# Plain 256-column runs instead of four-element pieces in the gate and query products of a two-block transformer kernel

## What is computed

```python
def odd_layer(h, norm_g, w_in, rpb, w_out):
    b, L, _ = h.shape
    u = rmsnorm(h, norm_g)
    proj = jnp.einsum("bld,de->ble", u, w_in)          # 272 x 2048 by 2048 x 8192
    q, k, v, z = split_cols(proj, (NA_WIDTH,) * 4)
    shp = (b, L, NA_HEADS, NA_HEAD_DIM)
    o = neighbourhood_attention(q.reshape(shp), k.reshape(shp), v.reshape(shp), rpb)
    o = o.reshape(b, L, NA_WIDTH) * jax.nn.silu(z)
    return h + jnp.einsum("ble,ed->bld", o, w_out)
...
    h = rmsnorm(h, final_norm_g)
    return h[:, N_META:]
```

## Time and profile before

| | before |
|---|---|
| median of three runs | 2334.29 us |
| the profiled execution | 2334.73 us |
| its span in the trace | 2332.9 us |
| PE busy | 2311.9 us (99%) |
| PE weight load busy | 2192.8 us (94%) |
| DVE busy | 1801.6 us (77%) |
| ACT busy | 1198.6 us (51%) |
| GpSimd (POOL) busy | 583.8 us (25%) |
| HBM read | 434.88 MB, 191 GB/s over the span |

### The profile page before, as it was taken

One profiled execution on the slowest core, in us unless ns is written; L12 is line 12 of the kernel. 1 busy time (PEld: TensorE's weight loads), 2 busy tenths in 40 slices (PEclk: granted clock), 3 DMA queues, 4 the chain that ended last, 5 costly groups with the idle time before them and its releaser, 6 DMA issues.

```text
span 2332.9 us, 51145 instructions
## 1 busy us (share of the span) xinstructions
PE 2311.9 (99%) x17404; PEld 2192.8 (94%) x17404; DVE 1801.6 (77%) x3189; ACT 1198.6 (51%) x1735; POOL 583.8 (25%) x421
## 2 busy tenths in 40 slices
PE   9999999999999999999999999999999999999997
PEld 9999888888888888899999999999999999999997
DVE  7777888888888766689888889989873566666666
ACT  5444455555555444457666743343544444444444
POOL 0230000000000000013423368888788211111100
PEclk9999999999999999999999999999999999999999
DMA  8544656666665666655555545555555554555444
GB/s 312 187 166 145 200 199 209 207 204 205 202 209 201 211 197 195 193 186 194 178 187 173 189 169 180 180 180 198 175 180 180 191 174 164 169 169 180 160 164 152
DMA packets 152908, 438.19 MB, mean 188 GB/s; under 512 B 32387, under 2 KB 47148, under 8 KB 152700
## 3 DMA queue, kind: packets, MB, share of 16 engines
q1 hardware_dynamic: 149276, 424.42, 53.7%
q0 software_dynamic: 3264, 12.41, 2.0%
q10 hardware_dynamic: 288, 0.30, 0.0%
HBM read 434.88 MB, written 11.09 MB: 191 GB/s over the span
## 4 chain that ended last, share of the span: by engine, by line
PE 85%; DVE 8%; issue 3%; ACT 3%; DVEq 1%; DMA 0%; ACTq 0%; SPq 0%
PE bank L1194 24%; PE bank L1177 15%; PE bank L1179 14%; PE bank L1178 14%; PE bank L1195 12%; DVE wlo L1657 2%; DVE c L2084 1%; ACT whi L680 1%; DVE bank L2310 1%; PE bank L1440 1%; PE bank L1560 1%; PE bank L1550 1%; PE bank L1540 1%; PE bank L1567 0%; ACT L663 0%
## 5 line engine op out<-in xcount | busy, mean ns | idle before, releaser
L680 ACT CAST whi<-raw 128x1024 fp32r<-128x1024 f32 x784 | 817.2, 1048 | 508.1 <-PE bank L1179 359.1
L1657 DVE TENSOR_TENSOR wlo<-raw,whi 128x1024 fp32r<-128x1024 f32 x624 | 761.8, 1226 | 224.7 <-ACT whi L680 210.9
L1177 PE MATMUL bank<-xhl,whi 128*128 128x272 f32 (+1 forms) x3024 | 859.3, 284 | 1.2 <-DVE nvt L2456 0.4
L1179 PE MATMUL bank<-xhl,wlo 128*128 128x272 f32 (+1 forms) x3024 | 848.9, 281 | 0.0
L1178 PE MATMUL bank<-xhl,whi 128*128 128x272 f32 (+1 forms) x3024 | 848.6, 281 | 0.0
L1177 PEld LDWEIGHTS bank<-xhl,whi 128*128 128x128 f32 x3024 | 567.7, 188 | 5.1 <-issue 2.2
L1178 PEld LDWEIGHTS bank<-xhl,whi 128*128 128x128 f32 x3024 | 567.8, 188 | 0.6 <-issue 0.2
L1179 PEld LDWEIGHTS bank<-xhl,wlo 128*128 128x128 f32 x3024 | 567.6, 188 | 0.0
L1194 PE MATMUL bank<-xhl,whi 128*128 128x512 f32 x1408 | 469.9, 382 | 0.3 <-DVE ug L1987 0.3
L618 POOL TENSOR_TENSOR wlo<-raw,whi 128x1024 fp32r<-128x1024 f32 x160 | 381.5, 2392 | 94.9 <-ACT whi L680 94.8
L1195 PE MATMUL bank<-xhl,wlo 128*128 128x256 f32 x1408 | 384.4, 273 | 0.0
(11 more groups left out here) (292 smaller groups left out, 2781.4 us busy)
## 6 DMA issues: line engine op xcount, KB each, us to landing
raw<-w_up SPq DMA_DIRECT2D x176, 512.0 KB, 4.3
raw<-w_na SPq DMA_DIRECT2D x128, 512.0 KB, 3.6
raw<-w_ssm SPq DMA_DIRECT2D x96, 512.0 KB, 3.7
raw<-w_glu SPq DMA_DIRECT2D x96, 512.0 KB, 3.6
raw<-w_down SPq DMA_DIRECT2D x80, 512.0 KB, 3.7
raw<-w_qkv SPq DMA_DIRECT2D x48, 512.0 KB, 3.7
raw<-w_mix SPq DMA_DIRECT2D x32, 512.0 KB, 3.7
raw<-w_outa SPq DMA_DIRECT2D x32, 512.0 KB, 3.6
```

Source lines behind the costliest of these rows:

```text
L680: A.copy(whi[s][:, :], raw[s][:, :]).then_inc(sem("hi_done"), 1)
L1177: T.matmul(to_, wh, xh_, start=head, stop=False)
L1179: ins = T.matmul(to_, wl, xh_, start=False, stop=last)
L1657: V.tensor_tensor(wlo[s][:, :], raw[s][:, :], whi[s][:, :].bitcast(F32), SUB).then_inc(sem("lo_done"), 1)
```

## The change

In `product`, the products of stage `na` whose width is 256 (the gates and the queries) are now read from `xhl` and summed in PSUM in one plain run of 256 columns. Before, they were walked by lines. The values and keys of that stage (272 columns) and all other stages are as before. No instruction is added or removed, and no wait.

```diff
--- before.py
+++ after.py
@@ -1172,7 +1172,7 @@
                     wh, wl = whi[s][:, r * P:r * P + P], wlo[s][:, r * P:r * P + P]
                     head, last = start and n_ == 0, stop and n_ == len(kts) - 1
                     to_, xh_, xl_ = out, mh[:, o:o + n], ml[:, o:o + n]
-                    if phase not in ("pin", "qkv"):
+                    if phase not in ("pin", "qkv") and (phase, n) != ("na", SEQ):
                         to_, xh_, xl_ = by_lines(to_), by_lines(xh_), by_lines(xl_)
                     T.matmul(to_, wh, xh_, start=head, stop=False)
                     T.matmul(to_, wh, xl_, start=False, stop=False)
```

## The result

The changed kernel takes 2343.10 us (median of 8 runs, 2341.75 to 2344.85), the kernel before 2336.07 us (median of 8, 2333.92 to 2338.63; its first three runs were those shown ahead of the prediction). The ratio is 1.0031, with a 95% interval of 1.0022 to 1.0039. The change makes the kernel slower by about 7 us, outside the range that was predicted. The profiled execution took 2343.36 us with a span of 2341.6, 8.7 us more than the span before.

What follows compares the result with a forecast made beforehand. PE was taken as the bound, so time follows matmul steps. A gain of 0.105 us a pass over 16 passes gave 1.7 us, taken as 1.6: 2334.29 - 1.6 = 2332.7 us (median), range 2331.5 to 2338.0.

Steps and rivals of the forecast that it cites:

- What bounds the kernel: PE busy without a gap in `na` at full clock, so each ns won per matmul is won on the path.
- What a plain run costs: Plain 256-column matmuls in `na` take 113.3 ns each as in `pin`, or 117.7 in the slow rhythm of `qkv`.
- the chunk after the transposes: 24 matmuls in each `na` pass after line 1550: 2.82 to 2.84 us against 2.84, gain taken as 0.005 us.
- Rival 2: Run of 72 in `na` locks in the slow rhythm: 3.2 us slower, 4.4 with slow chunk; chance 0.18.
- 8.47 us means rival 2: Sign in PE's timeline: 72-runs of `na` at 8.47 us, not the forecast 8.17, would show the slow rhythm.
- the last sentence of the prediction: Forecast is wrong if the plain run's step is neither 113.3 nor 117.7 ns, or if PE begins to wait.
- Rival 1: Quick run of 72 but slow chunk after the transposes in `na`: gain 0.5 us, no change, 2334.0 us; chance 0.27.
- Rival 3: Following stage `naout` falls to the slow pair rhythm: some 210 pairs at 9.2 ns more, 1.9 us; chance 0.07.
- Rival 4: Plain run in `na` cheaper than in `pin`, without the fixed 6.7 ns: gain 12.4 us, 2321.9; chance 0.01.
- whole cachelines: Walking costs nothing in itself, since four elements at a time are whole 8-byte PSUM cachelines.
- The range: Kernel time from 2331.5 to 2338.0 us, put at 0.84; the forecast's own part 2331.5 to 2333.5.

Runs made afterwards that it cites:

- one_line_lower: Changed kernel with the plain gates and queries of `na` read from one line (16 columns) lower, tokens 0 to 255; 2338.24 us, ratio to before 1.0014.
- sums_only_walked: Changed kernel with only the PSUM sums of the gates and queries walked by lines, columns read plainly; 2342.49 us in one run.
- reads_only_walked: Changed kernel with only the reading of the gates' and queries' columns walked by lines, sums written plainly; 2337.60 us in one run.
- weights_up_a_line: Changed kernel with the two weight rings moved up one line (64 bytes) against all other tiles; 2361.79 us, ratio 1.011.
- columns_up_a_line: Changed kernel with the activations of the later layers laid one line further up in their tile; 2341.36 us in one run.

## Why the prediction was wrong

**What bounds the kernel** held. PE has no gap in the stage in either kernel, the clock is the same, and each ns a step went straight into the time: 16 x 0.52 = 8.3 us of the 8.7 us that `na` grew by.

**What a plain run costs** is the step that failed. I read 113.3 ns in `pin` and, in `qkv`, the two rhythms of 113.3 and 117.7, and put them on `na` as all that a plain run can do. But all 30 entries that I went through lie in one tile at one distance from the weights, three lines and so odd. They were 30 samples of one case. The run in question starts at an even distance. The shift by one line alone takes the run of 72 in `na` from 8.65 to 8.48 us and 72 steps of `pin` from 8.16 to 8.54. That `T0` is three lines where `LINES` is two stood in the code that I had read. The term was 16 x (8.17 - 8.27) = -1.6 us and measured 16 x (8.65 - 8.27) = +6.1 us; the chunk after the transposes was put at a gain of 0.005 us a pass and measured 16 x (2.96 - 2.84) = +1.9 us. The sample was thin in another way too: lines 1262 and 1268, which gave the quick rhythm only, gave the slow one three times in the same `qkv` in the trace of after.

**Rival 2** had the right place and the right form, a steady slow rhythm that the walked reading doesn't fall into, but not the cause: it made it a matter of the entry. Its price was the slow rhythm of the wrong distance: 4.4 us at the most. The line "8.47 us means rival 2" would have read as neither; the last sentence of the prediction, a step that is neither 113.3 nor 117.7, is what came. Its argument against, that the 272s run without a collision and so PE enters without one, didn't help: the 120 ns came after those 272s and after the transposes (2.96 us), and after plain 272s it was still 118.6.

**Rival 1** was right that the run and the chunk can differ (one_line_lower has 117.8 and a quick chunk), the other way round. **Rival 3** didn't come: `naout` kept its rhythm. (It has 240 pairs and not some 210, so its price should have been 2.2 us.) Its half of the idea, that pairs know two rhythms, is seen in `mix`. **Rival 4** is refuted by the result. By the Trainium skill's rule ("PSUM — Partial Sum Buffer", specifications) the change would have been a gain. That it cost 7 us could have hidden a gain on the writing side; `sums_only_walked` and `reads_only_walked` exclude it. The reason that the prediction gave, whole cachelines, was tried by no run.

**The range** was too narrow for one reason: it took the worst row of a sample as the worst case. What no row showed was a plain run at this distance, and I had noted that only for the entry.

**What stays open.** What picks between the rhythms of one distance isn't settled. `one_line_lower` and `weights_up_a_line` lock the run of 72 at 117.8 ns, `columns_up_a_line` at 113.3, all three at an odd distance, and the second of them has both in one trace. Counted on a grid of four lines from the weight rings, `columns_up_a_line` and `weights_up_a_line` even stand at the same place, three lines, so a coarser grid of four doesn't explain it. Nor is it shown why 256 plain columns are quick at an odd distance and 272 aren't; 272 plain columns at an even distance were never run. That reading and weight load collide inside the memory is an inference from what moves the rhythm; no row shows a collision. What is shown is that the distance decides which rhythms appear.

## What to carry to other kernels

Where PE is full, the place of the moving columns against the weights loaded beside them is worth 6% of a matmul's cost here, so a step read in one stage can be carried to another only at the same distance, and even then with all the rhythms seen there, and a sample of thirty from one tile is a sample of one. Look at every offset in the code that seems arbitrary before you take a row for a law, and let one experiment shift it. Split an access pattern's change in its reading and its writing side: here one of them was worth all and the other nothing.

## What the runs showed of the hardware

- With fp32r operands and three matmuls for each weight piece, a plain run of 256 columns took 113.3 or 117.7 ns a step at an odd distance in 64-byte lines from the weights, 118.6 or 120.0 ns at an even one, 119.9 half a line off. Walked in pieces of four it took 114.9 at an even and 116.0 at an odd distance.
- For 272 columns at an odd distance, walking took 120.0 and plain reading 126.7 ns.
- Identical code falls into different rhythms from one profiled execution to another. In `mix`, which the change doesn't touch, 24 pairs take 8.22 us before and 8.00 in the profile of after:

```profile
260.24 0.38 PE L1194 MATMUL bank<-fhl,whi 128*128 128x512 f32 x1
...
268.24 0.38 PE L1194 MATMUL bank<-fhl,whi 128*128 128x512 f32 x1
```

  In `outb`, 72 of the walked 272-column matmuls take 8.64 us in the kernel before and 8.80 in `one_line_lower`, whose code is the same there:

```profile
1790.21 0.28 PE L1177 MATMUL bank<-ybh,whi 128*128 128x272 f32 x1
...
1798.85 0.28 PE L1177 MATMUL bank<-ybh,whi 128*128 128x272 f32 x1
```

```profile
1790.21 0.29 PE L1177 MATMUL bank<-ybh,whi 128*128 128x272 f32 x1
...
1799.01 0.29 PE L1177 MATMUL bank<-ybh,whi 128*128 128x272 f32 x1
```

  Over the whole stage it makes 1.5 us in `mix`, which seven of the twelve other traces have shorter than before by this amount, and 1.6 to 1.9 us in `outb`, longer in five of them. The runs of the kernel before scatter over 5 us; these two stages can hold 3 of them.
